# Attention heads of a hybrid RG-LRU and differential-attention layer: convolution one head ahead, rotation from row-exchanged loads, both recurrence directions together, a new order of steps

## The reference, cut to what matters

```
xc = centred_conv(xr, conv_w, conv_b)                 # 4 taps, depthwise
for d in (forward, backward):
    r, i = sigmoid(xc @ wr[d] + br[d]), sigmoid(xc @ wi[d] + bi[d])
    log_a = -8 * r * softplus(-lam[d]);  a = exp(log_a)
    h[d] = scan(a, sqrt(-expm1(2 * log_a)) * (i * xc))
y = (h[0] + h[1]) * gelu(gr)
q, k = apply_rope(q), apply_rope(k)                   # latent tokens; x1*cos - x2*sin, x2*cos + x1*sin
p = softmax(q1 k1^T / 8) - lam * softmax(q2 k2^T / 8) # differential attention
o = rmsnorm(p @ v) * 0.8
```

## Time and profile before

| | |
|---|---|
| runs (3) | 3135.09, 3138.99, 3139.11 us; median 3138.99 us |
| profiled execution | 3135.01 us, its span 3133.5 us, so 1.5 us lie around the span |
| busy share of the span | PE 93%, PEld (weight loads) 74%, DVE 68%, ACT 50% |
| head loop | 8 heads, from about 753 us to about 1430 us of the span |

### The profile page before, as it was taken

How to read it: one execution, slowest core, us unless ns; L and a number is a source line. 1 busy time by engine, 2 the same in 40 slices (tenths; PEclk the granted TensorE clock), 3 DMA queues, 4 the chain that set the end, 5 groups by cost and what they waited for, 6 DMA issues and landing times.

```text
span 3133.5 us, 42475 instructions
## 1 busy us (share of the span) xinstructions
PE 2922.5 (93%) x15736; PEld 2323.9 (74%) x15736; DVE 2146.1 (68%) x1829; ACT 1566.3 (50%) x1483; POOL 260.1 (8%) x294
## 2 busy tenths in 40 slices
PE   6899999998999999998998997799999999999993
PEld 2489999997888888887997876566666666666662
DVE  6636797794565556664334357788888888888885
ACT  5641212212445554553223245577777777777773
POOL 1000000002111111100000000000110000010100
PEclk9999999998999999999999998899999999999996
DMA  9646696693333233325433375799999999999995
GB/s 351 233 151 224 205 287 211 208 290 99 106 102 103 88 105 97 105 72 164 130 117 123 127 263 202 274 377 389 375 382 372 397 391 380 389 381 377 384 393 205
DMA packets 291187, 754.07 MB, mean 241 GB/s; under 512 B 19488, under 2 KB 183928, under 8 KB 226328
## 3 DMA queue, kind: packets, MB, share of 16 engines
q1 hardware_dynamic: 266768, 638.80, 56.3%
q0 software_dynamic: 21920, 98.56, 9.8%
q10 hardware_dynamic: 2432, 15.83, 1.2%
HBM read 696.86 MB, written 56.25 MB: 240 GB/s over the span
## 4 chain that ended last, share of the span: by engine, by line
PE 70%; DVE 14%; ACT 6%; issue 5%; DMA 4%; POOLq 0%; POOL 0%; DVEq 0%; ACTq 0%; SPq 0%
PE ps L415 15%; PE ps L416 15%; PE ps L417 15%; PE ps L1759 4%; PE ps L1760 4%; PE ps L1761 4%; DVE mod_acc L1253 3%; PE ps L1893 2%; PE ps L1892 2%; PE ps L1894 2%; PE ps L1684 2%; DVE w_lo L348 1%; DMA mod_raw<-in_w_mod 1%; ACT w_hi L339 1%; PE ps L1851 1%
## 5 line engine op out<-in xcount | busy, mean ns | idle before, releaser
L373 DVE TENSOR_TENSOR we_lo<-raw,we_hi 128x2048 fp32r<-128x2048 f32 x384 | 876.2, 2290 | 140.1 <-ACT we_hi L368 139.1
L368 ACT ACTIVATE we_hi<-raw 128x2048 fp32r<-128x2048 f32 x384 | 736.8, 1919 | 288.5 <-PE ps L417 288.5
L1759 PE MATMUL ps<-hi,w_lo 128*128 128x320 f32 x2048 | 650.7, 318 | 9.1 <-DVE m_row L1274 5.3
L1760 PE MATMUL ps<-lo,w_hi 128*128 128x320 f32 x2048 | 636.1, 311 | 0.0
L1761 PE MATMUL ps<-hi,w_hi 128*128 128x320 f32 x2048 | 635.8, 310 | 0.0
L348 DVE TENSOR_TENSOR w_lo<-raw,w_hi 128x2048 fp32r<-128x2048 f32 (+1 forms) x184 | 351.2, 1919 | 273.8 <-ACT w_hi L339 267.0
L339 ACT ACTIVATE w_hi<-raw 128x2048 fp32r<-128x2048 f32 (+1 forms) x184 | 294.4, 1612 | 309.4 <-PE ps L417 185.9
L1759 PEld LDWEIGHTS ps<-hi,w_lo 128*128 128x128 f32 x2048 | 388.0, 189 | 30.3 <-issue 23.0
L415 PE MATMUL ps<-we_hi,xs_lo 128*80 128x512 f32 x1024 | 402.6, 393 | 2.2 <-DVE xs_lo L1615 2.2
L416 PE MATMUL ps<-we_lo,xs_hi 128*80 128x512 f32 x1024 | 403.2, 394 | 0.0
L417 PE MATMUL ps<-we_hi,xs_hi 128*80 128x512 f32 x1024 | 400.6, 391 | 0.0
(11 more groups left out here) (345 smaller groups left out, 3763.0 us busy)
## 6 DMA issues: line engine op xcount, KB each, us to landing
raw<-in_w_e_gate SPq DMA_DIRECT2D x128, 1024.0 KB, 7.2
raw<-in_w_e_up SPq DMA_DIRECT2D x128, 1024.0 KB, 7.5
raw<-in_w_e_down SPq DMA_DIRECT2D x128, 1024.0 KB, 12.2
raw<-in_w_in SPq DMA_DIRECT2D x144, 512.0 KB, 5.1
mod_raw<-in_w_mod SPq DMA_DIRECT2D x64, 1024.0 KB, 5.3
raw<-in_w_mod SPq DMA_DIRECT2D x64, 512.0 KB, 5.2
raw<-in_w_o SPq DMA_DIRECT2D x64, 512.0 KB, 4.7
d_proj<-stage POOLq DMA_DIRECT2D x32, 320.0 KB, 3.2
```

The lines of the kernel that those rows point to most:

```text
L368: act.activation(we_hi[:, k % NEH, :], raw_slot(k), ACT.Copy).then_inc(hi_ready, 2)
L373: TTn(we_lo[:, k % NEH, :], raw_slot(k), we_hi[:, k % NEH, :].bitcast(F32), ALU.subtract).then_inc(lo_ready, 2)
L1759: pe.matmul(out, wl, hi[:, k, ms], start=(k % 16 == 0), stop=False)
L1760: pe.matmul(out, wh, lo[:, k, ms], start=False, stop=False)
```

## The change

- **Convolution.** It leaves the start of the head. The convolution of head h+1 runs in four steps on DVE, one behind each of the score tiles 1 to 4 of head h. The parameters of head h+1 are copied behind tile 0. The last head is written out behind the loop.
- **Rotation.** The permutation matmuls and their matrix are gone. `load_head` loads keys and queries a second time, as four blocks of 32 rows each with neighbouring blocks exchanged (`k_turn`, `q_turn`). That makes 15 transfers instead of seven. `rotate` multiplies these copies.
- **Recurrence.** Both directions have buffers of their own. ACT does the sigmoids of both, then exponentials and tangents of both, then square roots of both; DVE squares both before it scans both. Results are written in place (`gr` holds the GeLU, `li0` the forward scan and y).
- **Order of steps.** `keys` stands behind piece 0 instead of 2, the recurrence behind 1 and 2 instead of 3 and 4, `scores(0)` behind 5 instead of 7, `scores(1)` behind 7 instead of 9; the others keep about their places, and `turn_probs(4)` moves behind piece 14.
- **Start.** The 12 small loads go behind head 0's loads, the rotary tables too; PE no longer waits for the last modulation row before the head loop.

In PE's order the pieces of the filler are left out here; the rows show what stands at `keys`, `lru(0)`, `lru(1)` and the first two score tiles, in the kernel before. `ps` is PSUM, `k_past` the cached keys, `probs` the probabilities.

The diff, cut to its core (`split_lo`, `take`, `settle` and the like are as before; buffers are placed so that `rsd` lies in `probs`):

```diff
-        C = place(s0, [("rope", [P, 2, N_LAT], F32), ("perm", [P, P], F32), ("q_in", [P, N_TOK], F32),
+        C = place(s0, [("rope", [P, 2, N_LAT], F32), ("k_turn", [P, N_LAT], F32), ("q_turn", [P, N_LAT], F32),
+                       ("q_in", [P, N_TOK], F32),
...
-                         ("lr", "li", "la", "lt", "ld", "h_f", "h_b", "gel")])
+                         ("lr0", "la0", "ld0", "lr1", "la1", "li0", "li1", "ld1")])
...
-            for i, (g, gain) in enumerate(((4, "g_pre2"), (2, "g_post1"), (5, "g_post2"))):
-                for v in range(2):
-                    sl = slice(32 * i + 16 * v, 32 * i + 16 * v + 16)
-                    pool.dma_start(vec_rows[sl, :], flat(d_mod[v, g * D:(g + 1) * D])).then_inc(S["vrow_loaded"], 16)
-                    pool.dma_start(gain_rows[sl, :], flat(a[gain][0])).then_inc(S["vrow_loaded"], 16)
-
             pool.wait_ge(S["zero_stored"], TT * 16)
             change(pool, 2)
...
-            for name in ("rope", "perm"):
-                pool.dma_start(C[name][:], a[name]).then_inc(S["rope_loaded"], 16)
-
             def load_head(h):
 
-                for name, n, ready in (("xr", 0, "xr_loaded"), ("k", 24, "k_loaded"), ("q_in", 16, "q_loaded")):
+                pool.dma_start(C["xr"][:], d_proj[bass.ds(h * P, P), :]).then_inc(S["xr_loaded"], 16)
+                for name, turned, n, ready in (("k", "k_turn", 24, "k_loaded"), ("q_in", "q_turn", 16, "q_loaded")):
                     pool.dma_start(C[name][:], d_proj[bass.ds((h + n) * P, P), :]).then_inc(S[ready], 16)
+                    for r in range(0, P, HD // 2):
+                        pool.dma_start(C[turned][r:r + HD // 2, :],
+                                       d_proj[bass.ds((h + n) * P + (r ^ (HD // 2)), HD // 2), 0:N_LAT]).then_inc(S[ready], 16)
...
             load_head(0)
+            pool.dma_start(C["rope"][:], a["rope"]).then_inc(S["rope_loaded"], 16)
             load_values(0)
+            for i, (g, gain) in enumerate(((4, "g_pre2"), (2, "g_post1"), (5, "g_post2"))):
+                for v in range(2):
+                    sl = slice(32 * i + 16 * v, 32 * i + 16 * v + 16)
+                    pool.dma_start(vec_rows[sl, :], flat(d_mod[v, g * D:(g + 1) * D])).then_inc(S["vrow_loaded"], 16)
+                    pool.dma_start(gain_rows[sl, :], flat(a[gain][0])).then_inc(S["vrow_loaded"], 16)
...
-                    if d:
-                        act.wait_ge(S["lru_b"], h * 2 + d)
                     for i, dst in ((0, "lr"), (1, "li")):
-                        act.activation(halves(L[dst][:]), ps[:, 2 * i:2 * i + 2, 0:HALF], ACT.Sigmoid,
+                        act.activation(halves(L[f"{dst}{d}"][:]), ps[:, 2 * i:2 * i + 2, 0:HALF], ACT.Sigmoid,
                                        bias=C["prm"][:, (BR, BI)[i] + d:(BR, BI)[i] + d + 1]).then_inc(S["lru_sig"], 1)
-                    if d:
-                        act.wait_ge(S["lru_scan"], h * 2 + d)
+                def lru_decay(d):
                     act.wait_ge(S["lru_sig"], h * 4 + 2 * d + 2)
-                    act.activation(L["la"][:], L["lr"][:], ACT.Exp, scale=C["prm"][:, NEG + d:NEG + d + 1]
+                    act.activation(L[f"la{d}"][:], L[f"lr{d}"][:], ACT.Exp, scale=C["prm"][:, NEG + d:NEG + d + 1]
                                    ).then_inc(S["lru_at"], 1)
-                    act.activation(L["lt"][:], L["lr"][:], ACT.Tanh, scale=C["prm"][:, LAM_ + d:LAM_ + d + 1]
+                    act.wait_ge(S["lru_at"], h * 4 + 2 * d + 1)
+                    act.activation(L[f"lr{d}"][:], L[f"lr{d}"][:], ACT.Tanh, scale=C["prm"][:, LAM_ + d:LAM_ + d + 1]
                                    ).then_inc(S["lru_at"], 1)
                 def lru_root(d):
                     act.wait_ge(S["lru_q"], h * 2 + d + 1)
-                    act.activation(L["lt"][:], L["ld"][:], ACT.Sqrt).then_inc(S["lru_sqrt"], 1)
+                    act.activation(L[f"lr{d}"][:], L[f"ld{d}"][:], ACT.Sqrt).then_inc(S["lru_sqrt"], 1)
...
                 split_hi(act, Q_GATE + h, 1)
                 act.wait_ge(S["prm_set"], h + 1)
                 take(0, 0)
+                lru_gates(0)
+                lru_gates(1)
                 take(0, 1)
-                lru_gates(0)
+                lru_decay(0)
+                lru_decay(1)
+                take(1, 0)
+                split_hi(act, Q_GATE + h, 2)
                 lru_root(0)
-                split_hi(act, Q_GATE + h, 2)
-                take(1, 0)
-                lru_gates(1)
                 lru_root(1)
                 act.wait_ge(S["gr_loaded"], h * 16 + 16)
-                act.activation(L["gel"][:], C["gr"][:], ACT.Gelu_apprx_tanh).then_inc(S["gelu_done"], 1)
+                act.activation(C["gr"][:], C["gr"][:], ACT.Gelu_apprx_tanh).then_inc(S["gelu_done"], 1)
                 take(1, 1)
...
+            taps = ((0, -2), (1, -1), (3, 1))
+            def parameters(n):
+                dve.tensor_copy(prm[:, 0:NPRM], prm_all[:, bass.ds(n, 1), :].rearrange("p o m -> p (o m)")
+                                ).then_inc(S["prm_set"], 1)
...
+            def conv(n, step):
+                if step == 0:
+                    dve.wait_ge(S["prm_set"], n + 1)
+                    dve.wait_ge(S["xr_loaded"], n * 16 + 16)
+                    for b, e in spans:
+                        own.done(TS(xc[:, b:e], xr[:, b:e], prm[:, CW + 2:CW + 3], prm[:, CB:CB + 1], ALU.mult, ALU.add))
+                    return
+                tap, off = taps[step - 1]
+                own.settle()
+                for b, e in spans:
+                    d0, d1 = (b - off, e) if off < 0 else (b, e - off)
+                    last = STT(xc[:, d0:d1], xr[:, d0 + off:d1 + off], prm[:, CW + tap:CW + tap + 1],
+                               xc[:, d0:d1], ALU.mult, ALU.add)
+                    if tap == 3 and e == N_TOK:
+                        last.then_inc(S["xc_ready"], 1)
+                    else:
+                        own.done(last)
...
+            parameters(0)
+            for step in range(4):
+                conv(0, step)
+            def head(h, final):
                 split_lo(dve, Q_GATE + h, 1)
...
+                def rotate(i, x, turned, loaded, dst):
+                    dve.wait_ge(S[loaded], h * 80 + 80)
+                    own.done(TTn(x[:, 0:N_LAT], x[:, 0:N_LAT], C["rope"][:, 0, :], ALU.mult))
+                    TTn(turned[:], turned[:], C["rope"][:, 1, :], ALU.mult).then_inc(S["rot_read"], 1)
+                    dve.tensor_copy(dst[:, N_LAT:], x[:, N_LAT:]).then_inc(S["qk_ready"], 1)
+                    dve.wait_ge(S["rot_read"], h * 2 + i + 1)
                     own.settle()
+                    TTn(dst[:, 0:N_LAT], x[:, 0:N_LAT], turned[:], ALU.add).then_inc(S["qk_ready"], 1)
+                rotate(0, C["k"], C["k_turn"], "k_loaded", C["k_all"][:, PAST:])
+                rotate(1, C["q_in"], C["q_turn"], "q_loaded", C["q"])
...
+                def lru_square(d):
+                    lr, li, la, ld = (L[f"{n}{d}"][:] for n in ("lr", "li", "la", "ld"))
+                    dve.wait_ge(S["lru_at"], h * 4 + 2 * d + 2)
+                    own.done(TTn(ld, la, la, ALU.mult))
                     own.settle()
+                    STT(ld, ld, 1.0, lr, ALU.add, ALU.mult).then_inc(S["lru_q"], 1)
+                    own.done(TTn(li, li, xc[:], ALU.mult))
...
+                lru_square(0)
+                lru_square(1)
                 split_lo(dve, Q_GATE + h, 2)
-                lru(1)
-                own.done(TTn(L["h_f"][:], L["h_f"][:], L["h_b"][:], ALU.add))
+                lru_scan(0)
+                lru_scan(1)
+                y = L["li0"][:]
...
+                if not final:
+                    parameters(h + 1)
                 split_lo(dve, Q_GATE + h, 3)
                 for qt in range(1, TT):
                     row_max(qt)
                     differ(qt)
+                    if not final:
+                        conv(h + 1, qt - 1)
...
-                    pe.wait_ge(S["rope_loaded"], 32)
-                    pe.wait_ge(S["q_loaded"], h * 16 + 16)
-                    wait(pe, "o_ready", h * 2)
-                    for i, x in enumerate((C["k"], C["q_in"])):
-                        pe.matmul(ps[:, i, :], C["perm"][:], x[:, 0:N_LAT], start=True, stop=True
-                                  ).then_inc(S["rot_done"], 1)
                 def lru(d):
                     if d == 0:
                         pe.wait_ge(S["xc_ready"], h + 1)
                         pe.wait_ge(S["lruw_loaded"], h * 32 + 32)
-                        pe.wait_ge(S["rot_read"], h * 2 + 2)
+                        wait(pe, "o_ready", h * 2)
...
+                        pe.wait_ge(S["kt_taken"], h * 2 + 2)
...
-                after = {2: [keys], 3: [lambda: lru(0)], 4: [lambda: lru(1)], 7: [lambda: scores(0)],
-                         9: [lambda: scores(1)], 10: [lambda: turn_probs(0), lambda: scores(2)],
```

(74 more changed lines are left out.)

29 lines of the change are left out of this document (5 added, 24 removed).

## The result

The changed kernel takes 3151.4 us in the median of seven runs (3146.8 to 3156.6) against 3137.6 us (3135.1 to 3140.8) of the kernel before in as many: ratio 1.0044, 95% interval 1.0033 to 1.0056. The forecast was 3151. The profiled execution took 3150.5 us against 3135.0, 15.5 us more.

What follows compares the result with a forecast made beforehand. PE was taken to set the head loop's beat of 83.7 us. A median of 3139 plus 13 (+10 for eight heads, +3 at the start) gave 3152, stated as 3151 us, range 3135 to 3163.

Steps and rivals of the forecast that it cites:

- Full-clock head, 83.0 us: One head of the loop without clock loss: 82.8 - 1.7 - 4.6 - 0.5 + 7.0 = 83.0 us.
- the wait 7.0: PE at the second score tile waits 7.0 us in one piece for the exponentials of tile 0.
- y at t 37.7: Recurrence result y, which the first score exponentials wait for, ready 37.7 us after the head's piece 0 starts.
- rotation and its wait -3.1: On PE per head: 1.7 us of permutation matmuls and the 1.25 us wait of `lru(0)`, with some 0.15 resynchronising, go.
- What holds the pause: ACT's take of unit 1 and split of unit 2 hold the square roots, tying the recurrence to PE's pieces.
- faster rival: Take and split do not hold the roots: y 3.3 us earlier, pause 3.7, head 80.6, total 3117; chance 0.13.
- Half clock: Behind PE's pause at the second score tile: 4.4 us at 1.2 GHz, costing 2.0 us per head.
- The start: Ahead of the head loop, earlier loads but PE with more pieces left: +3 us, bounds 1.5 to 6.
- +1.9 for the keys: At the start: cached keys land 5.1 us earlier, at 758.8, but PE has 7.0 us of pieces left.
- +1 for the clock: At the start: half clock behind PE's long pause, 1.9 us, is no longer partly absorbed by the rotation wait.
- Convolution and doubled loads at 0 in the loop: DVE's convolution steps between score tiles and POOL's eight extra load issues, 4.5 us, are covered: 0 cost.

Runs made afterwards that it cites:

- e1: Changed kernel with 44 unused matmuls filling PE's pause ahead of the second score tile: 3135.0 us.
- e5: Kernel before with the change's rotation alone: no permutation matmuls, keys and queries loaded a second time with exchanged rows, nothing reordered: 3123.5 us.
- e2: Changed kernel with ACT's square roots and GeLU ahead of the take of unit 1 and the split of unit 2: 3123.1 us.
- e3: e2 with ACT's exponentials and tangents also ahead of the take of unit 0: 3123.3 us.
- e7: e3 with the first tile's score exponentials ahead of ACT's take of unit 1's second half: 3088.1 us.
- e9: e7 with the convolution back at the head's start, behind DVE's first split, none between score tiles: 3149.2 us.
- e4: Changed kernel with PE's old table of steps from the kernel before, all else changed: 3143.4 us.

## Why the prediction was right, point by point

- *Full-clock head, 83.0 us.* e1 has 82.8. The terms met it as well: the wait 7.0 (6.7 of idle time, 7.0 from the last start ahead of it to the first behind it), y at t 37.7 (37.6), rotation and its wait -3.1 (e5: -3.2).
- *What holds the pause.* Shown in part by e2: with the roots ahead it is 3.5 us. But behind that order lay a second hold of equal length, `take(1, 1)` ahead of the exponentials, that I had not seen; e3 and e7 show it. The faster rival's 3117 named the first hold alone, and e2 has 3123. Its pause was as that rival said (3.5 against 3.7), but not its clock: the rival let a pause under some 4 us cost no more than today's waits, and in e2 a slow stretch stood behind the pause in seven of eight heads.
- *Half clock.* The mechanism is shown by e1. The size was low: 5.5 us a head (5.3 to 5.7 in the eight) and not 4.4, so 2.5 us a head and not 2.0. Hence +1.6 a head and not +1.3: 13 us over eight heads, forecast 10 (counted head by head, 13.8, see the start).
- *The start.* Forecast +3, of which +1.9 for the keys and +1 for the clock. The keys landed at 757.0 and not 758.8: the first transfer was issued as forecast (748.4 against 748.9), but the landing came 2.7 us behind the issue and not 4.0. An estimate from the Trainium skill (DMA: Bandwidth & Descriptors, Anatomy of one DMA), 2.2, which I had set aside, was nearer here; e5 has 7.4 for the same transfer, so neither number is a rule for it. With 7.0 us of pieces still to do and a landing 6.9 earlier, the first term was +0.1. The clock's was +0.7: from the keys to the reciprocal, head 0 takes 1.5 us more than the third head in the changed kernel, and 0.9 more in the kernel before. The other 2.5 of the 3.3 us at the first reciprocal are head 0's own: 85.3 against 82.8, since in the kernel before head 0 has no slow stretch at its score tiles.
- *The hit to 0.4 us is luck.* In the profiles the eight heads cost 13.8 us (11.3 and head 0's 2.5), about 4 more than forecast, and the start 0.8, about 2 less, so two misses partly cancel. The forecast also stood on a median of 3139.0 from three runs, where seven give 3137.6: it said +12, and +13.8 was measured. That it lies in the stated range is not luck: the terms of the head and the mechanism came out as worked out.
- *Convolution and doubled loads at 0 in the loop.* Shown: in the changed kernel PE waits for neither, and e7 keeps both at a beat of 77.0. Put back (e9), the convolution costs 8.4 us a head in the order of e7; what its move is worth in the changed kernel's own order was not tested.

What stays open: e4 shows that the step order alone is not to blame, but the parts of the change were not taken out one by one from the changed kernel, and why the part behind the heads varies by up to 10 us is not known.

## What to carry to other kernels

When an engine's work is moved earlier, ask which in-order neighbour feeds it, and read that neighbour's list for instructions that wait for something later: here takes of gate banks and a split of weights stood ahead of work that was ready; changing three places in that list (and moving DVE's subtraction for the split along) took the beat from 85.3 to 77.0 us and turned +14 us into -51. A pause of PE can cost more than its length, since the clock is charged on top: 2.5 us a head behind 6.7 here. Cutting the pause in pieces is no cure by itself: e4's 3.1 and 2.1 us drew more slow time than the single 6.7, and e7's 0.9 and 0.4 drew none in any head. And when an experiment that removes a hold gains nothing more, read its timeline for a next hold of the same length.

## What the runs showed of the hardware that I had not expected

How much time at 1.2 GHz follows a pause of PE, in the 7 us behind it:

| idle time of PE | where | heads with a slow stretch | us at 1.2 GHz |
|---|---|---|---|
| 6.5 to 6.7 us | changed kernel | 8 of 8 | 5.3 to 5.7 |
| 6.1 to 6.3 us | e9 | 7 of 7 | 3.8 to 4.8 |
| 3.5 us | e2, e3 | 7 of 8 in each | 3.4 to 5.9 |
| 1.9 to 2.0 us, the second wait at the scores | kernel before, e5 | 4 and 5 of 8 | 3.4 |
| 0.7 to 0.9 us | e7 | none of 8 | 0 |

So the pause's length does not settle it alone: the same pause in the same kernel has a slow stretch in one head and none in the next. And matmuls whose results nobody reads, put into a pause, made this kernel 16 us faster (e1 against the changed kernel).
